# Four more of the conditioning units summed on VectorE, four more of the sums ahead of the attention turns

## The chip, the core and the metric

The kernel runs on one core of a Trainium2 chip. The metric is the device time of one execution in microseconds. Engines are named as in the profile: PE (TensorE, matrix products; PEld its weight loads), DVE (VectorE), ACT (ScalarE), POOL (GpSimd), and SP (SyncE, which here only issues transfers).

## The reference, cut to what matters

Two transformer-like blocks on 256 tokens of width 2048. Only the first block is touched by the change. Its conditioning vector and its attention part:

```python
cond = jax.nn.silu(c) @ w_ada[l] + b_ada[l]            # (1, 2048) @ (2048, 6 * 2048)
sh1, sc1, g1, sh2, sc2, g2 = [m[:, None, :] for m in jnp.split(cond, N_ADA, axis=-1)]
h = rmsnorm(x, norm1_g[l]) * (1.0 + sc1) + sh1
proj = h @ w_in[l]
...
y_ssm = s5_mixer(u_ssm, ...)      # ends in z * sigmoid(z @ w_glu + b_glu)
y_att = nsa_attention(q, ...)     # 8 heads of 128, two query blocks of 128
mixed = jnp.concatenate([rmsnorm(y_ssm, beta_ssm[l]), rmsnorm(y_att, beta_attn[l])], axis=-1)
x = x + g1 * (mixed @ w_out[l])
h2 = rmsnorm(x, norm2_g[l]) * (1.0 + sc2) + sh2
x = x + g2 * peer(h2, peer_w_q[l], ...)
```

The conditioning product is 12288 outputs, each a sum over 2048 inputs. `sh1` and `sc1` are needed at the very start, `g1` at the output product, `sh2`, `sc2`, `g2` later still.

## The kernel before

Weights come as units of 128 x 4096 f32 (2 MB) in a fixed stream. SP loads them into `ring`, four slots, in the order of use; a slot is filled again when PE has used it. The conditioning product is cut into 48 units of 256 outputs ("ada" units). 40 of them (ADA_ROWS) go through the ring and PE: `ada_rows(n)` (L797, L805) makes partial rows in psM or psW, ACT copies the row (`take_row`, L2304), and `ada_column(n)` (L810, L815) turns it into two columns. The other 8 (ADA_DOTS) have their weights transposed, with an output on each partition: such a unit is loaded whole into one of the two buffers `ada_raw` in `arena`, and DVE makes two sums of products of it, 128 outputs each (`ada_dot(d)`, L1633 to L1639; sum d uses unit d // 2 and buffer (d // 2) % 2). Loads 0 and 1 are issued by ACT before the turns. Load i from 2 on is issued by POOL (L2625 to L2627) when the sums of unit i - 2, the last reader of the buffer, have ended. Behind its loads POOL has a power for the SSM norm (L2629).

The attention runs in turns r = 0 to 18, one head and one query block each (`r // 2`, `r % 2`; an odd turn has twice the keys). Every engine has its turns written out, and every queue is in order.

- PE in turn r: the scores of r (L1045, L1047), the transposed probabilities of r - 2 (L1057, L1059), the attention output of r - 3 (L1072, L1075), and up to two fillers. In turns 0 to 3 these are two glu steps each (L977, 3.5 us apiece); from turn 4 on they are ada units 30 to 39. Turn 8 also has the SSM columns (L758), which wait for squares that DVE makes in turn 7, turns 15 and 17 a product over squares for a norm (L748). The scores of r wait for the logits of r - 2; glu step k waits until ACT has made k - 1 evictions (`glu_ev`), that is until step k - 2 is evicted, since two banks are in use. Behind turn 18 comes the column of the last ada unit and then w_out (L617).
- DVE: first four sums (DOTS_AHEAD), then in turn r the logits and their maxima (L1614 to L1621), the probabilities of r - 1 (L1627 to L1631), DOTS_AT[r] sums (L1639), and from turn 4 on a step of the SSM norm (`ssm_norm`, L1569 to L1584, and L1359, L1559, L1561).
- ACT in turn r: three exponentials (L2411) when the maxima are there, then the evictions of the fillers (`take_glu` L2321, `take_row` L2304), then copies of the transposed probabilities (L2422, L2423) and of the attention output (L2428). Ahead of turn 0 it evicts glu 0; glu 1 and 2 are evicted in turn 0, behind its exponentials.

```python
for d in range(DOTS_AHEAD):
    ada_dot(d)
for r in range(16 + 1):
    if r < 16:
        logits(r)
    if r >= 1:
        probs(r - 1)
    first = DOTS_AHEAD + sum(DOTS_AT[0:r])
    for d in range(first, first + DOTS_AT[r]):
        ada_dot(d)
    if r >= GLU_TURN:
        next(side)
```

Of the kernel before, what the change touches and what calls it, by code (L numbers as in the profile page):

```python
# [31 lines left out]
ALU = mybir.AluOpType  # L32
# [9 lines left out]
RING = 4  # L42
RAW = 2
ADA_UNITS = 48
ADA_ROWS = 40
ADA_DOTS = ADA_UNITS - ADA_ROWS
WSCALE = 256.0
HSCALE = 1 / 8
# [22 lines left out]
N_UNITS = 0  # L71
# [15 lines left out]
def scan_schedule():  # L87


    out, slot = [], 0  # L90
    pairs = {2 + round(1.25 * p): p for p in range(NSTATE_T // 2)}
    sums = {}
    for p in range(1, NSTATE_T // 2, 2):
        sums.setdefault(2 + round(1.25 * p) + 3, []).append(p // 2)

    def scan():
        nonlocal slot
        slot += 1
        if slot in pairs:
            out.append(("x", pairs[slot]))  # L100
        out.extend(("y", ct) for ct in sums.get(slot, []))
    for pos, v in enumerate(W_IN_ORDER):
        if pos:
            out.append(("ada", 15 + pos))
        out.append(("half", v))
        if pos:
            scan()
        if pos == 1:
            out.append(("gate_cols", 0))
        if pos:  # L110
            out.append(("column", 15 + pos))
        if pos == 11:
            out.append(("cmp_hid", 0))
        if pos == 12:
            out.append(("cmp_out", 0))
        out.append(("unit", v))
        if pos == 0:
            out.append(("gate_rows", 0))
        else:
            scan()  # L120
        if 7 <= pos <= 10:
            out.append(("cmp", pos - 7))
    assert sum(what == "y" for what, _ in out) == 8 and sum(what == "x" for what, _ in out) == 16
    return out
# [3 lines left out]
    ("w_in" if what == "unit" else what, n) for what, n in scan_schedule() if what in ("ada", "unit", "cmp")]  # L128
EARLY += [("ada", LATE_ADA), ("glu", 0), ("glu", 1)] + [("ada", n) for n in range(30, ADA_ROWS)]
UNIT_OF = {item: u for u, item in enumerate(EARLY)}  # L130
# [4 lines left out]
def slot_of(u):  # L135

    if u < SPLIT_0:
        return (u + 2) % RING, u // RING + 1
    return u % RAW, SPLIT_0 // RING + (u - SPLIT_0) // RAW + 1
# [46 lines left out]
def turn_fillers(r):  # L186

    if r < 4:
        return [("glu", 2 * r), ("glu", 2 * r + 1)]
    first = 30 + (10 * (r - 4) + 14) // 15  # L190
    return [("ada", n) for n in range(first, 30 + (10 * (r - 3) + 14) // 15)]


DOTS_AHEAD = 4
DOTS_AT = [0, 1, 1, 1, 1, 1, 1, 0, 1, 1, 1, 1, 0, 0, 0, 0, 2]
assert DOTS_AHEAD + sum(DOTS_AT) == 2 * ADA_DOTS


# [107 lines left out]
def program(nc, xT_d, wst, cst_d, dyn1_d, dyn2_d, dyn3_d, onehot_d, bmat_d, cmat_d, urow_d, vrow_d, skew_d, hrow_d, out_d):  # L306
    ctx = ExitStack()
    with ctx:
# [3 lines left out]
        def sem(name):  # L312
            return ctx.enter_context(nc.semaphore(name))
# [102 lines left out]
        minus_half = small[:, 60:62]  # L416
        rs_cols, rs_cols2 = small[:, 56:58], small[:, 58:60]
# [6 lines left out]
        ada_raw = [A[:, 0:4096], A[:, 8192:12288]]  # L424
# [53 lines left out]
        hi_done, split_done, lanes_ready, tab_ready = sem("hi_done"), sem("split_done"), sem("lanes_ready"), sem("tab_ready")  # L478
        split_half, half_used = sem("split_half"), sem("half_used")
        mod_sum = sem("mod_sum")  # L480
        c_row_ps, c_row_sb, ada_dots, ada_in = sem("c_row_ps"), sem("c_row_sb"), sem("ada_dots"), [sem(f"ada_in{i}") for i in range(ADA_DOTS)]
        route_hi, first1_ready = sem("route_hi"), sem("first1_ready")
        va_split, pool_split = sem("va_split"), sem("pool_split")
        h_tile, h_first = sem("h_tile"), sem("h_first")
# [8 lines left out]
        stat_sq, stat_used, stat_ms, stat_rs = sem("stat_sq"), sem("stat_used"), sem("stat_ms"), sem("stat_rs")  # L493
# [74 lines left out]
        def _(pe_):  # L568
# [241 lines left out]
            def ada_column(n):  # L810

                pe_.wait_ge(row_sb, n + 1)
                for m in range(2):
                    o = 384 + 2 * n + m
                    mm = nc.tensor.matmul(ada_bank(n)[:, o:o + 1], ada_row(n)[:, m * P:(m + 1) * P], lane_sum,  # L815
                                          start=True, stop=True)
                return mm
# [301 lines left out]

            ada_column(ADA_ROWS - 1).then_inc(mod_sum, 1)  # L1120
            pe_.wait_ge(mix_ready, 2)
# [192 lines left out]
        def _(v):  # L1314
# [82 lines left out]
            def par(k):  # L1397
                return J[:, 4096 + 32 * k:4096 + 32 * (k + 1)]
            dt, lrdt, th, rnd, r, co, cos, sin, w_re, w_im, pr, pi, q1, q2, q3, npr, npi = (par(k) for k in range(17))
# [223 lines left out]
            def probs(r):  # L1623
                h, qb = r // 2, r % 2
                nk, two, lc = views(r)
                v.wait_ge(exp_sb, 3 * (r + 1))
                step(v.reciprocal(smb[:, r % 3, :], smb[:, r % 3, :]))  # L1627
                step(tt(smb[:, r % 3, :], smb[:, r % 3, :], gates[:, qb, h, :], ALU.mult))
                for b in range(2):
                    D.put(ts(two[:, b, :], two[:, b, :], smb[:, r % 3, b:b + 1], None, ALU.mult))  # L1630
                stt(lc, lc, smb[:, r % 3, 2:3], cvalid[:, qb, :], ALU.mult, ALU.mult).then_inc(prob_sb, 1)  # L1631

            def ada_dot(d):  # L1633

                i, m = d // 2, d % 2
                v.wait_ge(ada_in[i], 16)
                raw = ada_raw[i % 2][:, m * HALF:(m + 1) * HALF]
                c = 2 * ADA_ROWS + d
                v.tensor_tensor_reduce(raw, raw, c_row, 1.0, 0.0, ALU.mult, ALU.add, mod[:, c:c + 1]).then_inc(ada_dots, 1)  # L1639

            side = ssm_norm()
            v.wait_ge(c_row_sb, 4)
# [10 lines that stand above are left out]
# [10 lines left out]
            v.wait_ge(mod_sum, 3)  # L1663
            dots_0 = 2 * ADA_ROWS
            late = 2 * LATE_ADA
# [914 lines left out]
        def _(g):  # L2580
# [23 lines left out]
            s, n = slot_of(UNIT_OF[("w_in", W_IN_ORDER[0])])  # L2604
# [19 lines left out]
                g.wait_ge(rotated, n + 1)  # L2624
            for i in range(2, ADA_DOTS):  # L2625
                g.wait_ge(ada_dots, 2 * i - 2)
                g.dma_start(ada_raw[i % 2], wst[N_UNITS + i, :, :]).then_inc(ada_in[i], 16)  # L2627
            g.wait_ge(stat_rs, 2)
            g.tensor_tensor(rs_cols, rs_cols, minus_half, ALU.pow).then_inc(stat_ms, 1)  # L2629
            g.wait_ge(att_sb, 16)  # L2630
            g.dma_start(X[:, :], xT_d.rearrange("p k t -> p (k t)")).then_inc(x_in, 16)
            g.dma_start(dyn[:, 0:256], dyn2_d).then_inc(dyn_in, 16)
# [88 lines left out]
def units_m(w):  # L2721

    n = w.shape[1]
    return w.reshape(16, P, n // 256, 2, P).transpose(2, 1, 3, 0, 4).reshape(n // 256, P, UNIT)
# [8 lines left out]
def units_b(w):  # L2733

    n = w.shape[1]
    return w.reshape(2, 32, P, n // P, P).transpose(3, 0, 2, 1, 4).reshape(2 * (n // P), P, UNIT)
# [7 lines left out]
def layout(i):  # L2744
# [18 lines left out]
        units_m(z), units_m(f["w_gate_2"][0]), units_m(abc), units_m(f["w_o_2"][0]),  # L2763
        units_m(f["w_up_2"][0]), units_b(f["w_down_2"][0]), units_d(f["w_ada"][0])[ADA_ROWS:]], axis=0)
    rcnt = np.zeros((4, 16), np.float32)
# [58 lines left out]
```

## Time and profile before

| | |
|---|---|
| median of 3 runs | 3171.46 us (3170.5 to 3174.11) |
| the profiled execution | 3170.16 us, its span 3168.4 us |
| PE busy over the span | 3121.3 us (99%) |
| DVE busy | 2299.5 us (73%) |
| ACT busy | 1250.5 us (39%) |
| POOL busy | 349.6 us (11%) |
| DMA | 821.25 MB, mean 259 GB/s |

Times in the rows are microseconds from the start of the span. A timeline row gives start, duration, engine, line, operation, what it writes and reads, its shape and the number of records in it; in brackets stands how long its engine was idle before it and what ended that. Several records of one kind that follow each other are merged in a row. An f32 product has two records. PE is shown busy for as long as matmuls are in flight, so its share says little; its starts say more.

### The profile page before, as it was taken

To read this page: it belongs to the slowest core of one execution; us is meant where nothing else is said; L and a number is where in the kernel's file an instruction comes from. 1 tells how busy PE (TensorE), PEld (TensorE's weight loads), DVE (VectorE), ACT (ScalarE), POOL (GpSimd) and SP (SyncE) were. 2 spreads that over 40 slices of the span, in tenths; PEclk is the share of its full clock that TensorE was granted. 3 is DMA by queue.
4 is the path that set the end of the run, shared out by engine and by line. 5 is a ranking of instruction groups with operands and counts; after the bars stand their busy time and mean duration, and the time that the engine had idled before them with its cause. 6 is when DMAs were issued, how large, how long until landed. Compare 5 with 4: busy or idle time off the path is not lost.

```text
span 3168.4 us, 65241 instructions
## 1 busy us (share of the span) xinstructions
PE 3121.3 (99%) x28144; PEld 2550.3 (80%) x28144; DVE 2299.5 (73%) x2792; ACT 1250.5 (39%) x1126; POOL 349.6 (11%) x292
## 2 busy tenths in 40 slices
PE   7999999999999999999999999999999999999998
PEld 4777878899996699679866668888888888876665
DVE  8586386799898877787798774698477756555554
ACT  2000143445444444444444454444443444443332
POOL 0266100000011221221111000300000000000000
PEclk9999999999999999999999999999999999999999
DMA  9858795556779999999898855655466555666653
GB/s 410 354 223 333 297 376 205 175 187 244 248 285 329 353 350 341 340 373 331 338 338 330 306 203 200 204 199 195 161 220 210 186 199 199 200 201 206 202 199 119
DMA packets 105282, 821.25 MB, mean 259 GB/s; under 512 B 12394, under 2 KB 14458, under 8 KB 15552
## 3 DMA queue, kind: packets, MB, share of 16 engines
q1 hardware_dynamic: 84960, 683.71, 60.0%
q0 software_dynamic: 17520, 128.11, 10.6%
q10 hardware_dynamic: 2592, 6.29, 0.5%
q8 instruction: 173, 2.83, 0.4%
q14 instruction: 37, 0.30, 0.0%
HBM read 814.00 MB, written 4.06 MB: 258 GB/s over the span
## 4 chain that ended last, share of the span: by engine, by line
PE 86%; DVE 11%; DMA 2%; issue 1%; ACT 0%; ACTq 0%; DVEq 0%; SPq 0%; POOLq 0%
PE psW L619 13%; PE psW L620 13%; PE psW L621 13%; PE psW L666 11%; PE psW L730 7%; PE psW L617 6%; PE psW L667 6%; DVE ring L1323 5%; PE psW L731 4%; PE psW L805 2%; PE psM L693 1%; PE psM L681 1%; PE psM L977 1%; PE psM L621 1%; PE psM L620 1%
## 5 line engine op out<-in xcount | busy, mean ns | idle before, releaser
L1323 DVE SCALAR_TENSOR_TENSOR ring<-ring 128x2048 f16<-128x2048 f32 x526 | 1200.5, 2290 | 532.5 <-ACT ring L2220 531.1
L2220 ACT ACTIVATE ring<-ring 128x2048 f16<-128x2048 f32 x526 | 1002.4, 1907 | 903.4 <-PE psW L621 400.3
L619 PE MATMUL psW<-h_act,ring 128*128 128x256 f16 (+1 forms) x5008 | 1324.7, 265 | 6.6 <-DVE ring L1323 5.5
L621 PE MATMUL psW<-h_act,ring 128*128 128x256 f16 (+1 forms) x5008 | 1324.1, 264 | 0.0
L620 PE MATMUL psW<-h_act,ring 128*128 128x256 f16 (+1 forms) x5008 | 1324.1, 264 | 0.0
L666 PE MATMUL psW<-arena,ring 128*128 128x416 f16 x2048 | 548.3, 340 | 3.7 <-DVE arena L1911 3.7
L619 PEld LDWEIGHTS psW<-h_act,ring 128*128 128x128 f16 x5008 | 489.8, 98 | 62.8 <-DVE ring L1323 11.3
L667 PE MATMUL psW<-arena,ring 128*128 128x208 f16 x2048 | 518.2, 253 | 0.0
L621 PEld LDWEIGHTS psW<-h_act,ring 128*128 128x128 f16 x5008 | 490.0, 98 | 33.5
L620 PEld LDWEIGHTS psW<-h_act,ring 128*128 128x128 f16 x5008 | 490.0, 98 | 33.5
L666 PEld LDWEIGHTS psW<-arena,ring 128*128 128x128 f16 x2048 | 200.6, 98 | 187.7 <-issue 17.2
L730 PE MATMUL psW<-arena,ring 128*128 128x512 f16 x1024 | 332.9, 379 | 0.0
L731 PE MATMUL psW<-arena,ring 128*128 128x256 f16 x1024 | 279.1, 273 | 0.0
L667 PEld LDWEIGHTS psW<-arena,ring 128*128 128x128 f16 x2048 | 200.7, 98 | 0.2
L730 PEld LDWEIGHTS psW<-arena,ring 128*128 128x128 f16 x1024 | 100.2, 98 | 120.7
L617 PE MATMUL psW<-h_act,ring 128*128 128x256 f32 x864 | 195.7, 382 | 0.0
L617 PEld LDWEIGHTS psW<-h_act,ring 128*128 128x128 f32 x864 | 162.0, 190 | 26.1 <-issue 5.2
L2640 POOL DMA_INDIRECT arena<-urow_dram,rs x48 | 113.2, 2357 | 342.0 <-DVE rs L1834 339.2
L1834 DVE CUSTOM_DVE_ANT_0 arena<-arena,proj 128x2048 f32<-128x2048 f32 x48 | 109.7, 2285 | 21.0 <-DMA arena<-urow_dram,rs 20.4
L2451 ACT ACTIVATE arena<-work 128x512 f16<-128x512 f32 x52 | 32.8, 630 | 206.9 <-DVE work L1905 196.3
L731 PEld LDWEIGHTS psW<-arena,ring 128*128 128x128 f16 x1024 | 100.2, 98 | 11.6
L2640 POOL DMA_INDIRECT proj<-vrow_dram,rs x48 | 61.9, 1290 | 404.4 <-PE psM L693 402.5
(445 smaller groups left out, 2669.2 us busy)
## 6 DMA issues: line engine op xcount, KB each, us to landing
ring<-wst_dram SPq DMA_DIRECT2D x522, 1024.0 KB
ring<-wst_dram SPq DMA_DIRECT2D x64, 2048.0 KB, 12.8
arena<-wst_dram POOLq DMA_DIRECT2D x6, 2048.0 KB, 14.7
proj<-h_rows POOLq DMA_DIRECT2D x6, 1024.0 KB
x_res<-xT_dram POOLq DMA_DIRECT2D x2, 2048.0 KB, 15.2
arena<-wst_dram ACTq DMA_DIRECT2D x2, 2048.0 KB, 14.7
out_dram<-x_res SPq DMA_DIRECT2D x4, 512.0 KB, 2.9
bias_rows<-proj POOLq DMA_DIRECT2D x1, 1536.0 KB, 26.2
```

Source lines behind the costliest of these rows:

```text
L617: return nc.tensor.matmul(out, ring[:, w0:w0 + P], rhs, start=first, stop=last)
L619: nc.tensor.matmul(out, whi(s, col, P), xh, start=first, stop=False)
L620: nc.tensor.matmul(out, whi(s, col, P), xl, start=False, stop=False)
L621: return nc.tensor.matmul(out, wlo(s, col, P), xh, start=False, stop=last)
L666: nc.tensor.matmul(psW[:, j, 0:2 * DENSE_T], whi(s, k * P, P), acts_x[:, a, k, :], start=(k == 0), stop=False)
L667: mm = nc.tensor.matmul(expert_sum(j)[:, 0, :, :], wlo(s, k * P, P), acts16[:, a, 0, k, :, :], start=False, stop=(k == QUART_T - 1))
L730: nc.tensor.matmul(psW[:, j // 2, :], whi(s, k * P, P), both, start=(j % 2 == 0 and k == 0), stop=False)
L731: mm = nc.tensor.matmul(psW[:, j // 2, 0:T], wlo(s, k * P, P), both[:, 0:T], start=False, stop=(j % 2 == 1 and k == 31))
L1323: ins = stt(wlo(s, c, n), ring[:, s * UNIT + c:s * UNIT + c + n], WSCALE, whi(s, c, n), ALU.mult, ALU.subtract)
L1834: v.tensor_tensor_reduce(row_buf[buf], row_buf[buf], h_rep, 1.0, 0.0, ALU.mult, ALU.add, dots[:, g, h:h + 1]).then_inc(dot_done, 1)
L2220: act(whi(s, p2 * (UNIT // 2), UNIT // 2), ring[:, c], ACT.Copy, scale=WSCALE).then_inc(hi_done, 1)
L2640: g.indirect_dma_start(row_buf[buf], None, (urow_d if kind == "u" else vrow_d)[:, :], bass.IndirectOffsetOnAxis(ap=row_index[:, i:i + 1], ...
```

## The change

ADA_ROWS goes from 40 to 36 and ADA_DOTS from 8 to 12. DOTS_AHEAD goes from 4 to 8, and the table DOTS_AT gets a sum in turn 7 and one in turn 12, and has four instead of two in turn 16. The ten ada fillers of PE become six, spread over the same turns. POOL's power for the SSM norm moves from behind all loads to behind load 9, and loads from 4 on share two semaphores.

```diff
-ADA_ROWS = 40
+ADA_ROWS = 36
...
-    first = 30 + (10 * (r - 4) + 14) // 15
-    return [("ada", n) for n in range(first, 30 + (10 * (r - 3) + 14) // 15)]
+    first = 30 + ((ADA_ROWS - 30) * (r - 4) + 14) // 15
+    return [("ada", n) for n in range(first, 30 + ((ADA_ROWS - 30) * (r - 3) + 14) // 15)]
...
-DOTS_AHEAD = 4
-DOTS_AT = [0, 1, 1, 1, 1, 1, 1, 0, 1, 1, 1, 1, 0, 0, 0, 0, 2]
+DOTS_AHEAD = 8
+DOTS_AT = [0, 1, 1, 1, 1, 1, 1, 1, 1, 1, 1, 1, 1, 0, 0, 0, 4]
...
-                v.wait_ge(ada_in[i], 16)
+                v.wait_ge(ada_in[i] if i < 2 else ada_in[2 + i % 2], 16 * max(i // 2, 1))
...
             for i in range(2, ADA_DOTS):
                 g.wait_ge(ada_dots, 2 * i - 2)
-                g.dma_start(ada_raw[i % 2], wst[N_UNITS + i, :, :]).then_inc(ada_in[i], 16)
-            g.wait_ge(stat_rs, 2)
-            g.tensor_tensor(rs_cols, rs_cols, minus_half, ALU.pow).then_inc(stat_ms, 1)
+                g.dma_start(ada_raw[i % 2], wst[N_UNITS + i, :, :]).then_inc(ada_in[2 + i % 2], 16)
+                if i == 9:
+                    g.wait_ge(stat_rs, 2)
+                    g.tensor_tensor(rs_cols, rs_cols, minus_half, ALU.pow).then_inc(stat_ms, 1)
```

On DVE, ahead of the logits of turn 0 (L1614), the order changes so; a sum is two rows, the product over a half buffer and the read of the accumulator:

```order
 L1639 ISA arena,mod<-arena 128x2048
 L1639 ISA mod 128x1
+L1639 ISA arena,mod<-arena 128x2048
+L1639 ISA mod 128x1
+L1639 ISA arena,mod<-arena 128x2048
+L1639 ISA mod 128x1
+L1639 ISA arena,mod<-arena 128x2048
+L1639 ISA mod 128x1
+L1639 ISA arena,mod<-arena 128x2048
+L1639 ISA mod 128x1
 L1614 SCALAR_TENSOR_TENSOR x_res<-psW,arena 128x2x128
 L1615 SCALAR_TENSOR_TENSOR x_res<-psM,cbias 128x15
```

Sums 4 to 7 now stand between sum 3 and the first logits.

On DVE in turn 16, behind the probabilities of turn 15 and ahead of the squares of the attention part (L1359):

```order
 L1639 ISA arena,mod<-arena 128x2048
 L1639 ISA mod 128x1
+L1639 ISA arena,mod<-arena 128x2048
+L1639 ISA mod 128x1
+L1639 ISA arena,mod<-arena 128x2048
+L1639 ISA mod 128x1
 L1359 TENSOR_TENSOR work<-proj 128x768
 L1359 TENSOR_TENSOR work<-proj 128x256
```

The squares come two sums later than they did.

On PE in turn 13, between the scores and the transposed probabilities of turn 11, a filler (column L815, rows L805) goes; the same happens in turn 17, and the earlier fillers stand in other turns:

```order
 L1045 MATMUL psW<-proj 128x256 x2
 L1047 MATMUL psM<-dyn,proj 128x15
-L815 MATMUL psM<-small,proj 128x1 x2
-L805 MATMUL psM<-ring,csilu 32x256 x16
 L1057 MATMUL psW<-ident,x_res 128x128 x4
 L1059 MATMUL psM<-ident,x_res 15x128
```

Turn 13 has no filler left.

## Rows read from the trace of the kernel before

**Rows 1.** Busy time by stretch, 10 us each; columns as its first line names them

```profile
core 0: us, PE busy (x) PEld busy (x) DVE busy (x) ACT busy (x) POOL busy (x), PEclk, DMA share, GB/s
...
410.00:420.00 10.00, 9.94 (x99) 7.96 (x102) 9.79 (x27) 5.74 (x26) 0.53 (x1) 1.00 0.99 422
...
430.00:440.00 10.00, 10.00 (x72) 8.43 (x71) 6.54 (x17) 2.29 (x9) 0.13 (x1) 0.66 1.00 428
```

**Rows 2.** Timeline of DVE, from the first sum to turn 4

```profile
361.62 2.29 DVE L1639 CUSTOM_DVE_ANT_0 arena<-arena 128x2048 f32<-128x2048 f32 x1
...
363.83 2.29 DVE L1639 CUSTOM_DVE_ANT_0 arena<-arena 128x2048 f32<-128x2048 f32 x1
...
372.88 0.43 DVE L1614 SCALAR_TENSOR_TENSOR x_res<-psW,arena 128x256 f32<-128x256 f32 x1 [2.33 <-PE psM L1047]
...
373.87 0.17 DVE L1621 TENSOR_SCALAR small<-small 128x3 f32<-128x3 f32 x1
...
406.40 0.42 DVE L1614 SCALAR_TENSOR_TENSOR x_res<-psW,arena 128x256 f32<-128x256 f32 x1 [4.34 <-PE psM L1047]
```

**Rows 3.** Timeline of PE: a glu pair, and turns 6 and 7

```profile
381.14 7.15 PE L977 MATMUL psM<-proj,ring 128*128 128x256 f32 x32
...
415.18 0.68 PE L1045 MATMUL psW<-proj 128*128 128x128 f32 x4
...
417.61 1.13 PE L1045 MATMUL psW<-proj 128*128 128x256 f32 x4
...
418.71 0.58 PE L815 MATMUL psM<-small,proj 128*128 128x1 f32 x4
419.23 1.93 PE L805 MATMUL psM<-ring,csilu 128*32 128x256 f32 x32
...
422.79 0.68 PE L1045 MATMUL psW<-proj 128*128 128x128 f32 x4
```

**Rows 4.** Timeline of DVE, turns 9 to 11 and the end

```profile
434.74 0.69 DVE L1614 SCALAR_TENSOR_TENSOR x_res<-psW,arena 128x512 f32<-128x512 f32 x1 [3.36 <-PE psM L1047]
...
439.57 0.41 DVE L1614 SCALAR_TENSOR_TENSOR x_res<-psW,arena 128x256 f32<-128x256 f32 x1
...
443.90 0.69 DVE L1614 SCALAR_TENSOR_TENSOR x_res<-psW,arena 128x512 f32<-128x512 f32 x1
...
448.66 0.42 DVE L1614 SCALAR_TENSOR_TENSOR x_res<-psW,arena 128x256 f32<-128x256 f32 x1
...
466.92 0.23 DVE L1631 SCALAR_TENSOR_TENSOR x_res<-x_res,small,cvalid 128x15 f32<-128x15 f32 x1
...
471.49 0.95 DVE L1359 TENSOR_TENSOR work<-proj 128x768 f32<-128x768 f32 x1
475.74 0.43 DVE L1359 TENSOR_TENSOR work<-proj 128x256 f32<-128x256 f32 x1 [3.30 <-ACT proj L2428]
```

**Rows 5.** Timeline of PE: the SSM columns, and the start of w_out

```profile
427.61 4.94 PE L758 MATMUL psM<-ones,work 128*128 128x1 f32 x32
...
475.79 3.70 PE L617 MATMUL psW<-proj,ring 128*128 128x256 f32 x16
```

**Rows 6.** POOL's load 3, its landing, and the landings of all six

```profile
370.85 0.54 POOL L2627 DMA_DIRECT2D arena<-wst_dram  x1 [3.55 <-DVE mod L1639]
...
arena<-wst_dram POOLq DMA_DIRECT2D x1, 2048.0 KB, 16.1
...
DMA to landing us min/median/max: 8.2/14.7/16.1
```

**Rows 7.** Timeline of ACT: exponentials of turn 0, eviction of glu 2

```profile
378.67 0.40 ACT L2411 ACTIVATE x_res<-x_res,small 128x128 f32<-128x128 f32 x1
...
379.65 0.19 ACT L2411 ACTIVATION_READ_ACCUMULATOR x_res<-x_res,small 128x1 f32 x1
...
384.88 0.47 ACT L2321 ACTIVATE arena<-psM,cst 128x256 f32<-128x256 f32 x1 [4.07 <-PE psM L977]
```

**Rows 8.** Timeline of PE behind an idle stretch, in a later stage

```profile
964.84 0.35 PE L666 MATMUL psW<-arena,ring 128*128 128x416 f16 x1 [3.71 <-DVE arena L1911]
...
966.02 0.55 PE L666 MATMUL psW<-arena,ring 128*128 128x416 f16 x1
```

More of the change, by code:

```diff
@@ L480, in program @@
         mod_sum = sem("mod_sum")
-        c_row_ps, c_row_sb, ada_dots, ada_in = sem("c_row_ps"), sem("c_row_sb"), sem("ada_dots"), [sem(f"ada_in{i}") for i in range(ADA_DOTS)]
+        c_row_ps, c_row_sb, ada_dots, ada_in = sem("c_row_ps"), sem("c_row_sb"), sem("ada_dots"), [sem(f"ada_in{i}") for i in range(4)]
         route_hi, first1_ready = sem("route_hi"), sem("first1_ready")
```

## The prediction

> **What bounds the kernel now.** I read the page's slices first, then the stretches around the attention turns, then the timelines of DVE, PE, POOL and ACT there. The change touches only the stretch from 361 us to about 476 us. Ahead of it both kernels do the same work in the same order, and behind it too, only shifted. So the question is by how much the start of the output product (w_out) moves.
>
> Between 410 and 420 us DVE is busy for 9.79 of 10 us, DMA is full, and PE is full by the page, though in small pieces [rows 1]. Three things are to be seen.
> First, in turns 0 to 3 PE is the bound: DVE waits for scores, 2.33 us at turn 0 and 4.34 us at turn 4 [rows 2], while the two glu steps of a turn take PE 7.15 us [rows 3].
> Second, from turn 4 on the two engines are nearly level. A turn with a filler (a conditioning unit on PE) costs PE 417.61 to 422.79 = 5.2 us, one without 415.18 to 417.61 = 2.4 us [rows 3]. On DVE an even turn with one sum takes 439.57 to 443.90 = 4.3 us, an odd one 443.90 to 448.66 = 4.8 us [rows 4]; 2.21 us of it is the sum, the step from one to the next being 361.62 to 363.83 [rows 2].
> Third, DVE has one real gap in turns 4 to 15, 3.36 us before turn 9, where PE did the SSM columns (4.94 us, partly at half clock), and one at the end, 3.30 us, where it waits for the last attention output [rows 4, 5].
>
> **The change part by part.**
> *Less work on PE.* Each of four units takes 32 records of rows (1.93 us) and a column (0.58 us) from it, 418.71 to 421.16 or 2.4 us [rows 3], together 9.8 us. Three of them leave turns 4 to 15, one leaves turn 17. The bytes are the same: a unit now comes to arena by POOL's queue and not to the ring by SP's.
>
> *Eight more sums on DVE*, 8 x 2.21 = 17.7 us: four ahead of turn 0, one each in turns 7 and 12, two in turn 16. It is more than PE gives back, but what counts is where each stands.
>
> *Ahead of turn 0.* Sums 4 to 7 need loads 2 and 3. POOL issues these as before, load 3 after sum 3 at 370.85, and it took 16.1 us [rows 6]; load 2 is issued 4 us earlier on the same queue. Until load 3 lands nothing else has changed, so I keep its 386.95. DVE does sums 4 and 5, waits, does 6 and 7 by 386.95 + 4.42 = 391.4, and only then takes the first logits, which it took at 372.88 before [rows 2]. Who waits? ACT is in order: glu 0 is evicted, next in its queue are the exponentials of turn 0, and behind these the evictions of glu 1 and 2. PE may start glu 3 only when glu 1 is evicted. Logits and maximum take 372.88 to 374.04, 1.2 us [rows 2], the exponentials 378.67 to 379.84, 1.2 us, an eviction 0.47 us [rows 7]. So glu 1 is evicted at 391.4 + 1.2 + 1.2 + 0.5 = 394.2. Before, PE started glu 3 at 384.8 (half-way in the pair that starts at 381.14 [rows 3]; ACT took glu 2 at 384.88 [rows 7]). PE stands for **9.4 us**. That DVE had idle time here is no help: PE is the bound in turns 2 and 3, so all of the 9.4 us arrives at turn 4.
>
> The 16.1 us is the landing of a load that shares the DMA engines. By the Trainium skill, DMA: Bandwidth & Descriptors, section Anatomy of one DMA, a transfer takes 2.0 us and its bytes at 436 GB/s, an estimate of 6.8 us for 2 MB. By that the early sums would run through to 386.4 and PE would stand for 4.4 us instead; the trace does not agree.
>
> *Clock after that wait.* PE idles 3.71 us before 964.84 and soon after works at half clock, products of 0.55 us instead of 0.35 [rows 8]. The only slow stretch inside the turns shows as a mean of 0.66 over 430 to 440 us [rows 1], which is 6.8 us at half clock. Half clock for 3.4 us, half of that, loses **1.7 us** and is what I take; bounds 0 and 3.4.
>
> *Turns 4 to 15.* DVE from the logits of turn 4 at 406.40 [rows 2] to the end of the last probabilities at 467.1 needed 60.7 us, without its gap of 3.36 us 57.3 [rows 4]; with two more sums 61.7. PE has twelve turns of 2.4 to 2.8 us, five fillers of 2.4 instead of eight, and the SSM columns, 4.9: some 48 us, and a few more for the norm's products. DVE is the bound, and PE's saving is worth nothing here. The gap does not go: sum 14 now stands in turn 7 ahead of the squares that the SSM columns wait for, so PE starts them later by as much. DVE has one even turn, 4.3 us, of work beside them; PE needs 3.6 us (full clock) to 4.9 us and 1.1 to 2.1 us for the scores: a wait of 0.4 to 3.4 us, and I take 2.0. The term is 4.4 - 3.4 + 2.0 = **3.1 us**, bounds 1.4 and 4.5.
>
> *Loads in turns 7 to 12.* Load i starts only after sum 2i-3 and is needed by sum 2i. DVE's turns leave 13.9 us for loads 7 and 8 and 11.8 us for load 9; landings are 8.2 to 16.1 us, median 14.7 [rows 6]. The waits would be 0 to 8.7 us in all. With fewer ring refills in these turns DMA is less full than before, so I take **1.0 us**.
>
> *Turn 16.* Behind the last probabilities DVE does its sums and then the second part of the squares; PE's product over these squares stands ahead of the last attention output. Before: probabilities to 467.1, two sums, squares to 472.44, then on PE the product, the attention output, the column, and w_out at 475.79 [rows 4, 5]. Two more sums are **4.4 us** on that path; the 3.30 us gap lies behind it and covers nothing, and the filler that left turn 17 is no gain, since PE waits there for the squares. PE now idles some 8 us ahead of them, so half clock once more, **1.7 us** (0 to 3.4).
>
> *Behind it* w_out runs on PE and all else hangs on it. POOL's power for the SSM norm stands behind load 9, issued after turn 8, ahead of its data: nothing.
>
> Sum: 9.4 + 1.7 + 3.1 + 1.0 + 4.4 + 1.7 = **21.3 us**. Against the profiled execution, 3170.16 us (span 3168.4), that is 3191.5; the median of the runs is 1.3 us above that execution, so **3192.8 us**, slower by 0.67%.
>
> **The rivals.**
> *A, faster: PE stays the bound throughout.* Four fillers less give 9.8 us, 3161.7 us. For it: PE is full in every stretch, and DVE has idle time before turn 4. Against it: the wait for load 3 moves the logits, not the sums' own time. It decides at glu 3: A needs glu 1 evicted before PE gets there, at 384.8.
> *B, the start as forecast, but PE paces turns 4 to 15:* 9.4 + 1.7 - 7.2 + 4.4 = 8.3 us, 3179.8 us. It needs DVE's rows to hide idle time, which rows 4 do not show.
> *C, no change: load 3 lands ten microseconds earlier and the start costs nothing,* the rest as in B: -7.2 + 4.4 + 1.7, about -1 us, 3170.
> *D, worse: the loads of turns 7 to 12 land at 14.7 us or later,* 6 to 9 us more, 3199 to 3202 us.
>
> **How the numbers follow.** Forecast 0.78, D 0.06, B 0.08, C 0.05, A 0.03. The forecast's own bounds run from 9.4 + 1.4 + 4.4 = 15.2 us (3186.7) to 9.4 + 3.4 + 4.5 + 3 + 4.4 + 3.4 = 28.1 us (3199.6), load waits above 3 us being D. The range reaches to B below and D above: 3179 to 3202. 0.2% is 6.3 us, about what a measurement of this kernel can tell from no change: slower (forecast, D, most of B) 0.90, same (C, the rest of B) 0.07, faster (A) 0.03.
>
> **What would show it.** DVE's seventh sum at 387 and the first logits at 391.4; ACT's eviction of glu 1 at 393.7; a gap of 9 us on PE before glu 3, scores of turn 4 at 416.7 instead of 405.6. Then DVE without gaps but one of some 2 us at turn 9, and probabilities of turn 15 ending near 482; PE idle 8 us before its product over the squares; w_out at 497. The prediction is wrong if PE has no gap at 385, or if w_out starts before 485.

## The result

The changed kernel takes **3198.26 us** (median of 4 runs, 3194.07 to 3199.86) against 3172.28 us (4 runs, 3170.5 to 3174.11) of the kernel before: ratio 1.008, interval 1.0062 to 1.0097. Slower by 26.0 us where 21.3 us were forecast: inside the range, 5.5 us above the forecast of 3192.8 us. The profiled execution took 3194.07 us, the lowest of the four, its span 3192.3 us.

The start, timelines of DVE, ACT and PE (these rows answer to [rows 2, 3, 7]):

```profile
376.95 2.29 DVE L1639 CUSTOM_DVE_ANT_0 arena<-arena 128x2048 f32<-128x2048 f32 x1 [6.40 <-DMA arena<-wst_dram]
...
386.74 2.29 DVE L1639 CUSTOM_DVE_ANT_0 arena<-arena 128x2048 f32<-128x2048 f32 x1 [5.28 <-DMA arena<-wst_dram]
...
391.17 0.42 DVE L1614 SCALAR_TENSOR_TENSOR x_res<-psW,arena 128x256 f32<-128x256 f32 x1
...
393.44 0.81 ACT L2321 ACTIVATE arena<-psM,cst 128x256 f32<-128x256 f32 x2
...
394.03 6.16 PE L977 MATMUL psM<-proj,ring 128*128 128x256 f32 x16 [9.19 <-ACT arena L2321]
...
417.53 0.61 PE L1045 MATMUL psW<-proj 128*128 128x128 f32 x4
```

DVE waits 6.40 us for load 2 and 5.28 us for load 3, takes the first logits at 391.17 instead of 372.88, ACT evicts glu 1 at 393.44, and PE has stood still for 9.19 us before glu 3. That glu step then takes 6.16 us for what takes 3.70 us at full clock.

Turns 7 to 10, timelines of DVE and PE (against [rows 4, 5]):

```profile
437.70 2.29 DVE L1639 CUSTOM_DVE_ANT_0 arena<-arena 128x2048 f32<-128x2048 f32 x1 [1.06 <-DMA arena<-wst_dram]
...
451.57 0.69 DVE L1614 SCALAR_TENSOR_TENSOR x_res<-psW,arena 128x512 f32<-128x512 f32 x1 [4.95 <-PE psM L1047]
...
458.97 0.42 DVE L1614 SCALAR_TENSOR_TENSOR x_res<-psW,arena 128x256 f32<-128x256 f32 x1 [2.48 <-PE psM L1047]
...
431.95 0.66 PE L1057 MATMUL psW<-ident,x_res 128*128 128x128 f32 x4 [1.19 <-DVE x_res L1631]
...
436.70 0.69 PE L1057 MATMUL psW<-ident,x_res 128*128 128x128 f32 x2 [2.25 <-DVE x_res L1631]
...
442.42 6.96 PE L758 MATMUL psM<-ones,work 128*128 128x1 f32 x32 [2.39 <-DVE work L1359]
449.24 2.05 PE L1045 MATMUL psW<-proj 128*128 128x256 f32 x4
...
452.30 3.64 PE L805 MATMUL psM<-ring,csilu 128*32 128x256 f32 x32
```

In turns 7 and 8, where two of the removed fillers stood, PE now waits 1.19 and 2.25 us for DVE's probabilities, then 2.39 us for the squares. The SSM columns take 6.96 us instead of 4.94, a filler's rows 3.64 instead of 1.93. After that DVE waits for PE, 4.95 us at turn 9 and 2.48 us at turn 10.

The filler at 451.38 to 455.87 (its column, L815, and its rows, L805) stands in turn 9 since the six fillers are spread anew. The kernel before has none there; timeline of PE in before, from the attention output of turn 9 to the scores of turn 10:

```profile
435.65 1.06 PE L1072 MATMUL psW<-x_res 128*128 128x128 f32 x4
...
437.07 0.71 PE L1045 MATMUL psW<-proj 128*128 128x128 f32 x4
```

Busy time in stretches of 10 us (PE, PEld, DVE, ACT and POOL with their numbers of instructions, granted clock, DMA share, GB/s; against [rows 1]):

```profile
390.00:400.00 10.00, 5.97 (x16) 4.91 (x17) 6.93 (x19) 3.16 (x14) 0.53 (x1) 0.55 0.85 343
...
430.00:440.00 10.00, 6.50 (x35) 5.38 (x34) 8.73 (x25) 4.10 (x17) 0.53 (x1) 0.83 1.02 437
440.00:450.00 10.00, 7.61 (x35) 7.52 (x35) 6.52 (x15) 1.45 (x7) 0.53 (x1) 0.50 0.62 223
450.00:460.00 10.00, 9.93 (x70) 7.10 (x68) 5.80 (x18) 3.04 (x12) 0.73 (x1) 0.65 0.69 256
490.00:500.00 10.00, 1.91 (x7) 1.45 (x7) 8.49 (x9) 0.65 (x3) 0.00 (x0) 0.56 0.27 115
```

There are three stretches at half clock (1.2 GHz). Cut to 1 us, the windows show 388.8 to 399.0, 436.6 to 457.1 and 491.2 to 501.4, that is 10.2, 20.5 and 10.2 us, where the kernel before had one of 6.8 us (429.9 to 436.7).

The end, and the first product of the later stage, timeline of PE (against [rows 5, 8]):

```profile
498.54 2.93 PE L748 MATMUL psM<-work,ones 128*128 128x256 f32 x6 [8.09 <-DVE work L1359]
...
503.21 3.70 PE L617 MATMUL psW<-proj,ring 128*128 128x256 f32 x16
...
990.42 0.35 PE L666 MATMUL psW<-arena,ring 128*128 128x416 f16 x1 [2.06 <-DVE arena L1911]
990.70 0.34 PE L666 MATMUL psW<-arena,ring 128*128 128x416 f16 x1
```

w_out starts at 503.21 instead of 475.79, 27.4 us later. The profiled execution ends only 23.9 us later. The 3.5 us come back around L666: PE waits 2.06 us there instead of 3.71, and finds full clock behind it (products of 0.34 us; [rows 8] has 0.55), where the kernel before has a mean clock of 0.66 over 965 to 970 us, 3.4 us at half clock, which is another 1.7 us. The other three runs are 3.8 to 5.8 us longer, and the medians differ by 26.0 us. What sets whether that comes back is open.

### The profile page after: what moved, and what is told of

Same layout as the page of the kernel before. It is cut to its first block, busy times and chain, and to the rows that moved or that the text cites. A ratio compares the mean times of both kernels' runs of the same rounds, so it can differ in the third digit from the quotient of the medians.

```text
span 3192.3 us, 64948 instructions
## 1 busy us (share of the span) xinstructions
PE 3121.3 (98%) x28000; PEld 2550.8 (80%) x28000; DVE 2317.2 (73%) x2808; ACT 1248.4 (39%) x1122; POOL 350.9 (11%) x296
## 4 chain that ended last, share of the span: by engine, by line
PE 82%; DVE 13%; DMA 3%; issue 1%; ACT 1%; DVEq 0%; ACTq 0%; SPq 0%; POOLq 0%
PE psW L619 13%; PE psW L621 13%; PE psW L620 13%; PE psW L666 11%; PE psW L730 7%; PE psW L617 6%; PE psW L667 5%; DVE ring L1323 5%; PE psW L731 4%; PE psW L805 2%; PE psM L693 1%; DMA ring<-wst_dram 1%; PE psM L681 1%; DMA arena<-wst_dram 1%; DVE arena L1639 1%
## 5 line engine op out<-in xcount | busy, mean ns | idle before, releaser
L666 PE MATMUL psW<-arena,ring 128*128 128x416 f16 x2048 | 546.6, 339 | 2.1 <-DVE arena L1911 2.1
L666 PEld LDWEIGHTS psW<-arena,ring 128*128 128x128 f16 x2048 | 200.2, 98 | 185.4 <-issue 16.9
## 6 DMA issues: line engine op xcount, KB each, us to landing
arena<-wst_dram POOLq DMA_DIRECT2D x10, 2048.0 KB, 12.1
x_res<-xT_dram POOLq DMA_DIRECT2D x2, 2048.0 KB, 14.2
arena<-wst_dram ACTq DMA_DIRECT2D x2, 2048.0 KB, 14.2
```

The source lines that it names most:

```text
L666: nc.tensor.matmul(psW[:, j, 0:2 * DENSE_T], whi(s, k * P, P), acts_x[:, a, k, :], start=(k == 0), stop=False)
```

## The experiments

The start of turn 0 differs between executions by up to 4.8 us in work that no kernel here changes (372.04 to 376.86). So each profile is read by a **stretch**: from PE's scores of turn 0 to its first product of w_out, cut at DVE's logits of turns 4 and 15. The three parts and the stretch are of one profiled execution each, the median is of all runs; all in us:

| kernel | median | ratio, interval | turns 0-4 | turns 4-15 | 15 to w_out | stretch |
|---|---|---|---|---|---|---|
| before | 3172.28 | | 34.4 | 55.2 | 14.2 | 103.7 |
| after | 3198.26 | 1.008, 1.0062-1.0097 | 46.3 | 64.9 | 20.0 | 131.2 |
| early_alone | 3181.19 | 1.0031, 1.002-1.0043 | 46.5 | 53.7 | 14.2 | 114.3 |
| ahead6 | 3186.33 | 1.0047, 1.003-1.0064 | 35.3 | 63.9 | 21.1 | 120.3 |
| ahead4 | 3191.91 | 1.0063, 1.0046-1.008 | 34.4 | 70.8 | 21.1 | 126.3 |
| tail_behind | 3188.51 | 1.0056, 1.004-1.0073 | 46.4 | 65.0 | 10.4 | 121.8 |
| turn7_behind | 3197.14 | 1.009, 1.007-1.0109 | 46.4 | 61.9 | 21.5 | 129.8 |
| awake | 3193.11 | 1.0072, 1.0054-1.009 | 44.0 | 64.7 | 18.6 | 127.4 |
| awake_ssm | 3196.7 | 1.008, 1.006-1.01 | 44.2 | 68.7 | 18.6 | 131.5 |
| sum7_to_13 | 3199.28 | 1.0082, 1.0065-1.0098 | 47.1 | 65.0 | 20.1 | 132.3 |
| awake_turns | 3201.72 | 1.0091, 1.0074-1.0108 | 43.9 | 67.8 | 18.6 | 130.3 |
| columns_turn9 | 3191.17 | 1.0059, 1.0043-1.0076 | 46.4 | 60.8 | 20.3 | 127.4 |
| best12 | 3181.2 | 1.0042, 1.0027-1.0057 | 37.7 | 61.2 | 10.4 | 109.3 |
| best12b | 3176.25 | 1.0014, 1.0004-1.0024 | 37.6 | 61.5 | 10.4 | 109.5 |

The kernel before ran beside each group: 3170.11 us (10 runs) beside the four from early_alone to tail_behind, 3170.18 (9 runs) beside turn7_behind, awake, awake_ssm and best12, 3172.58 (13 runs) beside the rest. A few terms of 1 to 2 us can be told in a profile's rows, not in the medians.

My theory at the outset was the prediction's sum: the early sums stop PE once, DVE paces turns 4 to 15, turn 16 puts its sums on the path, and each idle stretch is followed by half clock. The rivals were that the sums within the turns, not the early ones, cost most, and that the clock costs nothing of weight.

### The early sums alone

```diff
 (on the kernel before, eight units)
-DOTS_AHEAD = 4
-DOTS_AT = [0, 1, 1, 1, 1, 1, 1, 0, 1, 1, 1, 1, 0, 0, 0, 0, 2]
+DOTS_AHEAD = 8
+DOTS_AT = [0, 0, 0, 0, 0, 1, 1, 0, 1, 1, 1, 1, 0, 0, 0, 0, 2]
```

> The kernel before, eight units on VectorE as it was, with eight instead of four sums ahead of turn 0 and none in turns 1 to 4. The number of sums is that of before. Theory (the cost ahead of turn 0 is the wait for load 3, which keeps ScalarE from evicting glu 1, which keeps PE from glu 3): PE stands 9.2 us before glu 3, works at half clock behind it, and reaches the scores of turn 4 at 417.5 as in the changed kernel; 11.9 us over before, some 3184 us (3181 to 3187). Rival (the cost is the DVE time of the added sums, wherever they stand): same as before, 3172 us (3169 to 3175), since no sum is added.

Timeline of PE in early_alone, and its busy time over 430 to 440 us:

```profile
394.35 6.17 PE L977 MATMUL psM<-proj,ring 128*128 128x256 f32 x16 [9.40 <-ACT arena L2321]
...
439.84 3.73 PE L758 MATMUL psM<-ones,work 128*128 128x1 f32 x32
...
430.00:440.00 10.00, 9.94 (x110) 7.40 (x110) 9.72 (x29) 5.14 (x21) 0.53 (x1) 1.00 0.97 387
```

The time is in the range expected (3181 to 3187 us), against 3170.11 us of the kernel before beside it. The start costs what it costs in after: 46.5 against 46.3 us to the logits of turn 4, that is 12.1 us more than in before, with 9.40 us of standstill and half clock behind it. In the turns, where this kernel keeps its forty units on PE, nothing is lost. PE is full (9.94 of 10 us, after has 6.50), the columns run at full clock (3.73 us), and half clock shows for 3.4 us only, from 443 on. So **moving sums ahead costs 12.1 us at the start and nothing later**. 1.5 us of it come back in turns 4 to 15 here, since turn 4 has a sum less than in before, which leaves 10.6 us. The other 16.8 us of after come from the four units that moved and the sums they bring.

### Fewer sums ahead

```diff
 (ahead6)
-DOTS_AHEAD = 8
-DOTS_AT = [0, 1, 1, 1, 1, 1, 1, 1, 1, 1, 1, 1, 1, 0, 0, 0, 4]
+DOTS_AHEAD = 6
+DOTS_AT = [0, 2, 2, 1, 1, 1, 1, 1, 1, 1, 1, 1, 1, 0, 0, 0, 4]
 (ahead4)
+DOTS_AHEAD = 4
+DOTS_AT = [0, 2, 2, 2, 2, 1, 1, 1, 1, 1, 1, 1, 1, 0, 0, 0, 4]
```

> The changed kernel with six sums ahead instead of eight, the two others in turns 1 and 2. Theory: six sums need only load 2, they end at 381.4, glu 1 is evicted at 384.4 and glu 3 starts at 384.8 with no gap and full clock. The start term goes: scores of turn 4 near 406, w_out near 492, 3187 us (3184 to 3191). Rival (the sums' own DVE time is the cost): no sum is removed, 3198 us as changed (3195 to 3201).

> The changed kernel with four sums ahead, as before, and two each in turns 1 to 4. Theory: no gap at glu 3, as with six ahead, but turn 4, where VectorE is the bound, has one sum more: 2.2 us over the six-ahead kernel, 3189 us (3185 to 3193). Rival: 3198 us.

With six ahead the standstill before glu 3 is gone and turns 0 to 4 take 35.3 us: two sums may go ahead for 0.9 us; this went as expected (3186.33 us, 3184 to 3191 expected). With four ahead they take 34.4 as in before, but the loads fall behind. PE then waits once for 8.09 us in turn 7 for probabilities that stand behind a load. Timelines of DVE and PE in ahead4:

```profile
426.96 2.29 DVE L1639 CUSTOM_DVE_ANT_0 arena<-arena 128x2048 f32<-128x2048 f32 x1 [5.56 <-DMA arena<-wst_dram]
...
432.59 1.12 PE L1057 MATMUL psW<-ident,x_res 128*128 128x128 f32 x4 [8.09 <-DVE x_res L1631]
```

So the place of the sums can be too late as well as too early: turns 4 to 15 take 63.9 and 70.8 us. The time of ahead4 fell in the range expected (3185 to 3193 us), but partly by luck: turns 4 to 15 take 6.9 us more than in ahead6 where the theory had 2.2, and it did not have the wait behind the load at all.

### Turn 16

```diff
 (tail_behind: in turn 16, and behind the last squares)
+                if r in (16,):
+                    next(side)
                 for d in range(first, first + DOTS_AT[r]):
                     ada_dot(d)
-                if r >= GLU_TURN:
+                if r >= GLU_TURN and r not in (16,):
                     next(side)
...
             squares(2, lambda a, m: tiles(J, 8 + a, m), (2,))
+            for d in range(2 * ADA_DOTS - 2, 2 * ADA_DOTS):
+                ada_dot(d)
             inverse_rms(2)
```

DOTS_AT has two sums left in turn 16, and they come behind the squares.

> The changed kernel with the sums of turn 16 moved behind the squares of the second part: two there, and two behind the last squares, where VectorE waits for the norm's sum. Theory (all four sums of turn 16 stand on the path to PE's product over the squares): that product starts 8 us earlier, PE has no idle stretch of 8.1 us and no half clock there: 8.1 + 1.4 = 9.5 us less, 3189 us (3186 to 3191). Rival (the end of the turns is set by PE or by the last probabilities, and the sums there cost only 4.4 us, those that were added): 3194 us (3192 to 3196).

The last part fell from 20.0 to 10.4 us, the other two stayed, and the time is in the middle of the range expected. Timeline of PE in tail_behind:

```profile
494.93 1.56 PE L748 MATMUL psM<-work,ones 128*128 128x256 f32 x6
```

With the squares first there is no wait of 8 us ahead of this product and no half clock behind it. The four sums of turn 16, standing ahead of the squares, cost 9.6 us in after, half clock included; the two that the change adds are 5.8 us of it (20.0 against 14.2). The last part is also 3.8 us shorter than in before, so before's own two sums seem to stand in the way there too; moving them in that kernel was not tried.

### Turn 7

```diff
 (turn7_behind)
+                if r in (7,):
+                    next(side)
                 for d in range(first, first + DOTS_AT[r]):
                     ada_dot(d)
-                if r >= GLU_TURN:
+                if r >= GLU_TURN and r not in (7,):
                     next(side)
 (sum7_to_13)
-DOTS_AT = [0, 1, 1, 1, 1, 1, 1, 1, 1, 1, 1, 1, 1, 0, 0, 0, 4]
+DOTS_AT = [0, 1, 1, 1, 1, 1, 1, 0, 1, 1, 1, 1, 1, 1, 0, 0, 4]
```

> The changed kernel with the sum of turn 7 moved behind the squares that the SSM columns wait for. Theory (that sum delays the columns by its own 2.2 us, and VectorE then waits for the scores of turn 9): the columns start 2.2 us earlier, the 4.95 us wait before turn 9 shrinks by as much; 2 to 4 us less than the changed kernel, from the scores of turn 0 to w_out 127 to 129 us instead of 131.2. Rival (VectorE's total work sets the end whatever the order of these two): no change, 131 us.

> The after kernel with the new sum of turn 7 put in turn 13 instead, so that DVE makes the squares for the SSM columns right behind the probabilities of turn 6. Theory (the sum in turn 7 keeps PE waiting for the squares, PE falls to half clock, and the waits of turns 9 and 10 follow): turn 7 costs DVE 3.3 us less (sum and load wait), the wait for the scores of turn 9 goes back from 4.95 us to about 3.4 us, that of turn 10 from 2.48 us to 0, and turn 13 costs 2.2 us more. From the scores of turn 0 to w_out 131.2 - 3.3 - 1.6 - 2.5 + 2.2 = 126.0 us. Rival (PE is idle in these turns in any case, since DVE paces them, and the clock falls whatever stands ahead of the squares): PE at half clock for some 20 us from turn 8 on as in the after kernel, waits of 5 and 2.5 us stay, and only the load wait of 1.1 us goes, about 130 us.

In both PE no longer waits for the squares. Timelines of PE and DVE, the first two rows of turn7_behind, the others of sum7_to_13:

```profile
439.55 0.69 PE L1057 MATMUL psW<-ident,x_res 128*128 128x128 f32 x2 [2.25 <-DVE x_res L1631]
...
442.81 6.99 PE L758 MATMUL psM<-ones,work 128*128 128x1 f32 x32
...
442.30 0.58 PE L1057 MATMUL psW<-ident,x_res 128*128 128x128 f32 x2 [2.24 <-DVE x_res L1631]
...
445.45 6.99 PE L758 MATMUL psM<-ones,work 128*128 128x1 f32 x32
...
454.63 0.69 DVE L1614 SCALAR_TENSOR_TENSOR x_res<-psW,arena 128x512 f32<-128x512 f32 x1 [5.74 <-PE psM L1047]
```

The columns take 6.99 us all the same. In turn7_behind the turns gain 3.0 us: the columns and the logits of turn 9 come about 2.4 us earlier, counted from the logits of turn 4, and DVE's waits at turns 9 and 10 are 3.63 and 1.93 us instead of 4.95 and 2.48. But the half clock at the end lasts 17.1 us instead of 10.2, the last part takes 1.5 us more, and 1.4 us are left of the gain (129.8 us, 127 to 129 expected). It also reaches into w_out, whose first sixteen records take 5.15 us instead of 3.70. In sum7_to_13 nothing is left: turn 7 is 3.3 us shorter, then DVE waits 5.74 us at turn 9, since PE and not DVE sets when turn 9 starts, and the sum costs its 2.2 us in turn 13. It takes 132.3 us where 126.0 was expected.

So the sum ahead of the squares and its wait for the load do delay the columns, by 2.4 us, but **the theory that it causes the waits and the half clock falls**: both stay without it. The clock is already low when the columns begin (it fell at 439.2 in turn7_behind and at 442.5 in sum7_to_13), behind PE's waits in turns 7 and 8.

### PE kept busy where it waits

```diff
+            def hold_clock(bank, times):
+                for _ in range(times):
+                    nc.tensor.matmul(bank[:, 0:P], ident[:, :], ident[:, :], start=True, stop=True)
...
+                if r == 1:                                 # awake, awake_ssm, awake_turns
+                    hold_clock(psW[:, 3, :], 36)           # ahead of glu 3
+                if r in (7, 8):                            # awake_turns
+                    hold_clock(psM[:, 2, 256:384], {7: 5, 8: 10}[r])
...
                 if r == SSM_SUM_TURN:
+                    hold_clock(psM[:, 3, :], 9)            # awake_ssm, awake_turns
                     ssm_columns()
...
                 if r == 17:
+                    hold_clock(psW[:, 0, :], 32)           # awake, awake_ssm, awake_turns
                     stat_sum(2, (1,))
... (in ssm_columns, awake_ssm and awake_turns)
                     for k in range(8):
+                        if k % 2 == 0:
+                            nc.tensor.matmul(psM[:, 2, 256:384], ident[:, :], ident[:, :], start=True, stop=True)
```

> The changed kernel with idle PE time filled by products of the identity into unused banks: 36 ahead of glu 3 in turn 1 and 32 ahead of the product over squares in turn 17, both about as long as the waits there (9.2 and 8.1 us); nothing at the SSM columns. Their results are not used. Theory (the two idle stretches put PE at half clock behind them): both slow stretches go, 2.5 us at glu 3 and 1.4 us at the end, 127.3 us from the scores of turn 0 to w_out instead of 131.2. Rival (the half clock there costs nothing, VectorE is late anyway): 131 us; or slower by what the products overrun the waits.

> As the one before, and also nine such products ahead of the SSM columns and eight between them, since the columns alone (one column wide) seem to let the clock fall as an idle PE does. Their results are not used. Theory (the 20 us at half clock around the SSM columns are what made the waits before turns 9 and 10 4.95 and 2.48 us instead of the 2.0 forecast): the products cost 2 us, the waits shrink by about 5; some 124 us from the scores of turn 0 to w_out. Rival (the columns are slow by themselves, not by the clock): 2 us more than the run before, 129 us.

> The after kernel with identity products on PE wherever it waited: 36 ahead of glu 3, 5 ahead of the transposed probabilities in turn 7, 10 in turn 8, 9 ahead of the SSM columns and 8 between them, 32 ahead of the product over squares in turn 17. They change no result. Theory (the short waits of 1.2, 2.3 and 2.4 us in turns 7 and 8 let the clock fall, since the products at the columns alone did not help): no half clock between 430 and 460 us, the columns take about 4.6 us with the products between them instead of 7, and the waits of DVE for the scores of turns 9 and 10 fall from 4.95 and 2.48 us to under 3 and 0. From the scores of turn 0 to w_out about 127.4 (products at the long waits alone) - 4.5 = 123 us. Rival (the clock falls for what PE works on there, products of one column and of 15 and 128, and not for its waits): half clock stays for some 20 us and the stretch takes 127 to 132 us.

At the two long waits it went as expected. Timeline of PE in awake:

```profile
395.73 3.69 PE L977 MATMUL psM<-proj,ring 128*128 128x256 f32 x16 [1.39 <-ACT arena L2330]
...
497.60 1.56 PE L748 MATMUL psM<-work,ones 128*128 128x256 f32 x6 [0.75 <-DVE work L1368]
```

Glu 3 takes 3.69 us instead of 6.16, the product over squares 1.56 instead of 2.93, and the stretch 3.8 us less (127.4 us, 127.3 expected). Half clock behind these waits thus cost 2.2 us (46.3 to 44.0) and 1.4 us (20.0 to 18.6).

At the columns it failed twice: awake_ssm takes 131.5 us where 124 was expected, awake_turns 130.3 where 123 was. Timeline and busy time of PE in awake_turns:

```profile
444.97 0.46 PE L759 MATMUL psM<-ident 128*128 128x128 f32 x2 [1.73 <-DVE work L1372]
445.27 0.50 PE L760 MATMUL psM<-ones,work 128*128 128x1 f32 x4
...
452.93 0.78 PE L759 MATMUL psM<-ident 128*128 128x128 f32 x2
453.50 0.85 PE L760 MATMUL psM<-ones,work 128*128 128x1 f32 x4
454.21 2.05 PE L1047 MATMUL psW<-proj 128*128 128x256 f32 x4
...
430.00:440.00 10.00, 9.94 (x81) 8.79 (x74) 8.92 (x25) 5.00 (x20) 0.53 (x1) 1.00 1.01 428
...
446.00:454.00 8.00, 8.00 (x41) 8.00 (x40) 3.13 (x6) 1.10 (x6) 0.53 (x1) 0.50 0.49 168
```

Two things come apart here. Between 430 and 440 us, with turns 7 and 8 filled, PE is full again and at full clock, where after had 6.50 us of work and lost it at 436.6. So the waits of turns 7 and 8 are what lets it fall there (awake, which up to the columns lacks only these two fillings, fell at 434.9). But inside the columns it fell all the same, at 446.1, and came back at 463.1. PE was busy throughout from 445 on; a wait of 1.73 us stood just ahead, so this kernel alone does not say whether that or the columns did it. Before fell 2.3 us into its columns (429.9 against 427.61, [rows 5]) and early_alone at their end, both with no wait of PE ahead. The products that I put between them ran at half clock too and stretched the columns from 6.96 to 9.2 us (10.1 in awake_ssm), so the scores of turn 9 came later: DVE waits 7.37 us for them in awake_turns and 9.41 in awake_ssm. In awake_ssm turns 4 to 15 take 4.0 us more than in awake, in awake_turns 3.0. What a kernel with turns 7 and 8 filled and bare columns would take was not tried.

### The columns a turn later

```diff
-                if r == SSM_SUM_TURN:
+                if r == SSM_SUM_TURN + 1:
                     ssm_columns()
 (the spread of its result, and DVE's step that reads it, one turn later as well)
```

> The after kernel with the SSM columns on PE in turn 9 instead of turn 8, what hangs on them one turn later too. The squares are then ready and PE need not wait for them, and the scores of turn 9 stand ahead of the columns. Theory (the wait for the squares, and the columns behind it, is what stops DVE at turns 9 and 10): no wait of DVE before the logits of turn 9, at turn 10 between 0 (columns at full clock, 3.6 us) and 3 us (half clock, 7 us) instead of 2.48 us. From the scores of turn 0 to w_out 131.2 - 4.95 - 2.48 + 0 to 3 = 123.8 to 127 us. Rival (the columns' work only moves: PE has as much to do between two scores one turn later): the wait of 5 us comes at turn 10, and the stretch takes 130 us or more.

Timeline of PE and DVE in columns_turn9:

```profile
450.06 5.26 PE L758 MATMUL psM<-ones,work 128*128 128x1 f32 x32
...
456.66 0.42 DVE L1614 SCALAR_TENSOR_TENSOR x_res<-psW,arena 128x256 f32<-128x256 f32 x1 [3.39 <-PE psM L1047]
```

DVE no longer waits at turn 9 and waits 3.39 us at turn 10: 4.0 us less than 4.95 + 2.48, and turns 4 to 15 take 4.1 us less. Both sizes lie just outside what was expected (0 to 3 us of wait, 123.8 to 127 us of stretch, 127.4 measured). Now PE has no wait ahead of the columns, and its busy time in stretches of 1 us shows the clock by itself:

```profile
449.00:450.00 1.00, 1.00 (x9) 0.82 (x6) 0.96 (x5) 0.70 (x3) 0.35 (x1) 1.00 1.22 229
450.00:451.00 1.00, 1.00 (x11) 0.94 (x9) 0.93 (x7) 0.88 (x5) 0.00 (x0) 1.00 0.39 98
451.00:452.00 1.00, 1.00 (x12) 1.00 (x11) 1.00 (x2) 0.71 (x4) 0.00 (x0) 0.99 0.95 410
452.00:453.00 1.00, 1.00 (x7) 1.00 (x7) 1.00 (x1) 0.00 (x0) 0.00 (x0) 0.50 0.99 426
```

It had fallen at 438.3 behind the waits of 1.20 and 2.24 us in turns 7 and 8, was back at 448.6, and fell again at 452.0, 1.9 us into the columns, though PE had been busy without a break since 438.6. The kernel before shows the same without any wait, in its window of 1 us:

```profile
429.00:430.00 1.00, 1.00 (x10) 1.00 (x11) 1.00 (x3) 0.31 (x3) 0.00 (x0) 0.94 1.04 442
```

So **two things let the clock fall here**: the waits of turns 7 and 8, which awake_turns shows by filling them, and something in the columns. For the columns it is the place of the fall that speaks, inside them or at their end in three kernels with PE busy ahead; no run leaves them out. Where the waits come first, the low stretch begins before the columns and takes them in from their first product.

### Twelve units, arranged by what was learnt

```diff
 (best12)
-DOTS_AHEAD = 8
-DOTS_AT = [0, 1, 1, 1, 1, 1, 1, 1, 1, 1, 1, 1, 1, 0, 0, 0, 4]
+DOTS_AHEAD = 6
+DOTS_AT = [0, 2, 2, 2, 1, 1, 1, 1, 1, 1, 1, 0, 0, 0, 0, 0, 2]
 (best12b)
+DOTS_AT = [0, 2, 2, 2, 1, 1, 1, 1, 1, 1, 1, 1, 0, 0, 0, 0, 3]
 (both: next(side) ahead of the sums in turns 7 and 16; three, or one, sums behind the last squares)
```

> Twelve units on VectorE, but placed by what was learnt: six sums ahead, two in each of turns 1 to 3, one in each of 4 to 10, that of turn 7 behind the squares, none in turns 11 and 12, two in turn 16 behind the squares of the second part and three behind the last squares. Theory: no gap at glu 3, no sum on the path at the end; VectorE has 7 sums in turns 4 to 10 as before has in 4 to 11, so the turns cost what they did and a few us of waits for loads: 4 to 10 us over before, 3174 to 3180 us. Rival (with four fillers less PE is the faster and the kernel gains): 3166 us, faster than before.

> Twelve units as in the after kernel, arranged by what the earlier runs showed: six sums ahead, two each in turns 1 to 3, the norm's step ahead of the sums in turns 7 and 16, three sums in turn 16, and only one behind the last squares instead of three. Theory (what was left in the arrangement with three of them was a wait of 5.7 us for the norm of the attention part behind those sums): from the scores of turn 0 to w_out two sums more, 109.3 + 4.4 = 113.7 us, the wait for the norm under 1 us, total 3181.2 + 4.4 - 5.7 = 3179.9 us, still slower than the kernel before. Rival (PE is ahead again and the saving of four fillers shows): 3165 to 3170 us.

best12 brought w_out to 109.3 us, but its three sums behind the last squares, the first of which waits 3.50 us for its load, hold up the norm, and PE waits for that inside w_out. Its 3181.2 us are 1 us above the range expected. Timeline of PE in best12:

```profile
496.41 13.82 PE L617 MATMUL psW<-proj,ring 128*128 128x256 f32 x55 [5.72 <-DVE proj L1664]
```

best12b has no such wait. Two sums moved ahead of w_out again and cost it nothing (109.5 us; I had expected 4.4 us for them, and 3179.9 us in all). One stands in turn 11, where the turns take 0.3 us more; the other, behind the squares of turn 16, leaves the last part at 10.4 us. It takes 3176.25 us, ratio 1.0014, interval 1.0004 to 1.0024: by the ratios 0.66% or 21 us better than after, and 0.14% slower than before. No arrangement of twelve units here beats eight. What is left against before is 3.2 us in the start and 6.3 us in turns 4 to 15, less 3.8 us at the end.

## Why the prediction was right, and which term was too small

**Start.** Right. Landmarks forecast and measured: seventh sum 387 and 386.74, first logits 391.4 and 391.17, eviction of glu 1 393.7 and 393.44, standstill 9.4 and 9.19 us. early_alone repeats it with the number of sums unchanged (9.40 us). Load 3 landed as its row of before said [rows 6], not after the 6.8 us of the estimate that the prediction sets beside it. The 386.4 and 4.4 us worked out there do not follow from 6.8 us either: if load 2, issued at 366.71, took 6.8 us as well, the sums would end at 382.4 and PE would stand for about 0.5 us.

**Clock behind it.** Forecast 1.7 us, 2.2 us by awake against after and 2.5 us by glu 3's own row (6.16 against 3.70). Scores of turn 4: 417.53 instead of 416.7.

**Turns 4 to 15, with the loads.** This is the mis-sized term: 3.1 + 1.0 = 4.1 us forecast, 9.7 us measured (64.90 - 55.19). The two sums were right, 4.4 us, and the load wait too, 1.06 us. The rest is DVE's waits for PE: 4.95 instead of 3.36 us at turn 9, and 2.48 us at turn 10 (4.4 + 1.06 + 1.6 + 2.5 = 9.6 us). The step that failed is the one where PE needs "3.6 us (full clock) to 4.9 us" for the columns, so that the wait before turn 9 is 0.4 to 3.4 us. The columns took 6.96 us and the scores behind them 2.05, beside 4.3 us of DVE's work, and DVE waited 4.95 us. The upper bound was the slowest the columns had been in before, and before had its half clock only from 2.3 us into them. (From the prediction's own terms the upper end is 4.9 + 2.1 - 4.3 = 2.7 us, not 3.4.)

The second wait, at turn 10, the sum did not have at all. Between the scores of turns 9 and 10 PE now does a filler that was not there before, and does it at half clock: 451.38 to 455.87, 4.5 us, where a filler took 2.4 us in [rows 3]. Before had half clock in turn 9 too, but no filler and no wait. By these rows the wait of 2.48 us needs both; a spread of the six fillers with none in turn 9 was not tried.

I had written that PE's saving "is worth nothing here". It was worth less than nothing: the fillers that left turns 7 and 8 left waits of 1.19 and 2.25 us, and behind these the clock was down for 20.5 us instead of 6.8. early_alone keeps the fillers and has neither; turn7_behind and sum7_to_13, without the new sum ahead of the squares, still have both.

Of short idle periods the Trainium skill, TensorE: Matmul & The Clock Gate, section A second HAM failure mode: psum-queue depth-cycling (HAM is the page's name for what gates the clock), says that in a bf16 kernel with products of 512 columns TensorE pauses briefly between groups of products often enough for the clock to go back and forth. After's waits of 1.19 and 2.25 us, with f32 products between them and the fall at 436.6, agree with that; the fall inside the columns of columns_turn9, with no pause since 438.6, is not covered by it.

**Turn 16.** 4.4 us of sums right, as is PE's wait, 8.09 us; half clock behind it 1.4 us instead of 1.7 (awake), 5.8 us together instead of 6.1.

**Behind w_out.** Taken as a pure shift. In the profiled pair 3.5 us came back, in the medians 1.4 us (27.4 - 26.0). This hid part of the miss: w_out starts 27.4 us later, not 21.3 (503.21 where 497 was forecast).

**The rivals.** A and C needed the start to cost nothing, and PE stood there for 9.19 us. B and they needed four units less on PE to shorten turns 4 to 15, which grew by 9.7 us. D's times (3199 to 3202 us) nearly fit and its mechanism does not: the loads cost 1.1 us, not 6 to 9.

## What to carry to other kernels

Work taken off an engine that waits for another anyway does not always leave harmless idle time: if it is TensorE, the short waits that take its place can halve its clock, and then it becomes the bound at half speed. Before moving work, look at what its removal leaves idle and whether work follows that lets the clock fall by itself (here the SSM columns, products of one column). And of work that is put ahead of a shared queue's first item, count who stands behind it: a fifth and a sixth sum ahead cost 0.9 us, a seventh and an eighth brought it to 11.9 us, since they wait for a load, and ACT and PE then wait with them.

## What the runs showed of the hardware that I had not expected

- Sixteen f32 products with one column (L758, 32 records) take 3.73 us at full clock (early_alone) and 6.96 us at half (after), and the granted clock falls inside them or at their end with no wait of PE ahead (before, early_alone, columns_turn9).
- Identity products in a wait keep the clock up: 36 in the wait of 9.2 us and 32 in that of 8.1 us gave 3.8 us of the stretch back (awake). Between the columns they ran at half clock themselves and only added to the time.
- The same half clock can end in one kernel after 6.8 us and in another after 20.5 us. What lets it end sooner in before than in awake_turns (17.1 us, likewise begun inside the columns, with identity products between them) is open.
